# The last mixer's head loop: the second out-gate panel, the key drains and the decay scans in other places

## The reference

```
z = h @ w_in                      # q | k | v | out_gate
g = log_sigmoid(h @ down @ up + bias) / 16        # for each direction
per chunk of 64 tokens: b = cumsum(g)
  A = tril((q*exp(b)) @ (k*exp(-b)).T);  o = A @ v + (q*exp(b)) @ S
  S = exp(b_last) * S + (k*exp(b_last - b)).T @ v
o = rms_norm(o_fwd + o_bwd, g_norm) * silu(out_gate);  y = o[latent] @ w_o
```

## Time and profile before

| | us |
|---|---|
| median of 3 runs | 2536.21 (2536.12 to 2538.74) |
| profiled execution, its own time | 2537.61 |
| its span, first to last instruction | 2535.8 |
| mean granted TensorE clock | 0.988 |
| TensorE busy | 2421.2 (95%) |
| VectorE busy | 877.4 (35%) |
| ScalarE busy | 474.6 (19%) |

### The profile page before, as it was taken

The page is one execution under the profiler, slowest core; times in us unless marked ns, Lnnn a source line. Parts: engine busy times, 40 slices in busy tenths (PEclk is TensorE's granted clock), DMA queues, the critical chain, the costliest instruction groups (busy, mean ns, idle before and its releaser), DMA issues.

```text
span 2535.8 us, 23072 instructions
## 1 busy us (share of the span) xinstructions
PE 2421.2 (95%) x9410; PEld 1611.3 (64%) x9410; DVE 877.4 (35%) x1906; ACT 474.6 (19%) x971; POOL 69.6 (3%) x101
## 2 busy tenths in 40 slices
PE   6999999999999999999999998999999989878998
PEld 4888686886478867868846554444444454547843
DVE  4663312321246532133462766810000134533001
ACT  1222320100011223010102553211100032422100
POOL 1000000000010000000000000100000001000000
PEclk9999999999999999999999999999999999989999
DMA  9753334575375333447682004541212127033431
GB/s 391 284 203 116 133 117 149 193 264 209 149 266 211 121 133 117 155 173 268 214 294 100 34 34 142 183 150 67 75 66 99 67 91 271 12 108 134 165 141 66
DMA packets 163321, 390.92 MB, mean 154 GB/s; under 512 B 6288, under 2 KB 10768, under 8 KB 160400
## 3 DMA queue, kind: packets, MB, share of 16 engines
q1 hardware_dynamic: 134400, 276.61, 30.6%
q0 software_dynamic: 26256, 102.12, 10.9%
q10 hardware_dynamic: 2560, 10.72, 1.1%
HBM read 388.37 MB, written 1.05 MB: 154 GB/s over the span
## 4 chain that ended last, share of the span: by engine, by line
PE 92%; DVE 4%; ACT 3%; issue 1%; DMA 1%; POOL 0%; DVEq 0%; ACTq 0%; POOLq 0%
PE bank L455 91%; ACT arena L1182 2%; PE bank L453 2%; DVE arena L1712 1%; DVE arena L1706 1%; DMA arena<-in_w_ada 1%; ACT arena L1185 1%; DVE arena L1709 1%; ACT L1182 0%; DVE arena L1775 0%; DVE arena L2295 0%; DVE arena L1835 0%; DVE arena L2327 0%; POOL arena L2419 0%; DVE arena L2332 0%
## 5 line engine op out<-in xcount | busy, mean ns | idle before, releaser
L455 PE MATMUL bank<-arena 128*128 128x256 f32 (+6 forms) x8922 | 2365.7, 435 | 64.3 <-DVE arena L1709 29.1
L455 PEld LDWEIGHTS bank<-arena 128*128 128x128 f32 (+2 forms) x8922 | 1554.5, 189 | 862.2 <-issue 673.9
L1712 DVE SCALAR_TENSOR_TENSOR arena<-arena 128x1028 f32<-128x1028 f32 (+6 forms) x416 | 361.1, 881 | 456.5 <-ACT arena L1182 356.4
L1706 DVE TENSOR_TENSOR arena<-bank,arena 128x512 f32<-128x512 f32 (+3 forms) x115 | 78.6, 691 | 587.7 <-PE bank L455 578.3
L1185 ACT ACTIVATE arena<-bank 128x512 f32<-128x512 f32 x227 | 127.7, 597 | 730.7 <-PE bank L455 683.2
L1182 ACT ACTIVATE arena<-arena 128x512 f32<-128x512 f32 (+7 forms) x294 | 156.4, 552 | 439.8 <-DVE arena L1787 163.1
L1706 DVE TENSOR_TENSOR arena<-arena 128x1024 f32<-128x1024 f32 (+7 forms) x233 | 94.6, 424 | 328.1 <-DMA arena<-in_post 274.4
L1182 ACT ACTIVATE arena<-bank 128x512 f32<-128x512 f32 (+1 forms) x135 | 66.1, 505 | 751.1 <-PE bank L455 750.3
L2428 POOL DMA_DIRECT2D arena<-in_w_ada x88 | 63.0, 716 | 2226.4 <-DVEq L1721 2220.3
L1712 DVE SCALAR_TENSOR_TENSOR arena<-bank,arena 128x254 f32<-128x254 f32 (+3 forms) x208 | 96.1, 501 | 51.8 <-PE bank L453 35.8
L453 PE MATMUL bank<-arena 128*128 128x128 f32 x488 | 64.2, 281 | 40.9 <-DVE arena L1709 33.2
(11 more groups left out here) (29 smaller groups left out, 105.0 us busy)
## 6 DMA issues: line engine op xcount, KB each, us to landing
arena<-in_w_ada POOLq DMA_DIRECT2D x96, 1028.0 KB, 6.9
arena<-in_w_in SPq DMA_DIRECT2D x84, 1024.0 KB, 7.3
arena<-in_w SPq DMA_DIRECT2D x60, 1024.0 KB, 7.4
arena<-in_w_mlp_in SPq DMA_DIRECT2D x32, 1024.0 KB, 7.6
arena<-in_w_mlp_out SPq DMA_DIRECT2D x32, 1024.0 KB, 7.2
arena<-in_w_gla SPq DMA_DIRECT2D x12, 1024.0 KB, 7.3
arena<-in_w_a SPq DMA_DIRECT2D x8, 1024.0 KB, 6.9
arena<-in_w_out SPq DMA_DIRECT2D x8, 1024.0 KB, 6.2
```

Source lines behind the costliest of these rows:

```text
L455: ins = nc.tensor.matmul(out, lhsT, rhs, start=start, stop=stop)
L1706: return V.tensor_tensor(out, x, y, op)
L1712: return V.scalar_tensor_tensor(out=out, in0=x, scalar=s, in1=y, op0=op0, op1=op1, **kw)
```

## The change

`GLA_PANELS` now has the second out-gate panel (column 5) last. Its two tiles leave the front: GG 2 takes the place of a key tile at the start of head 3's turn, GG 3 stands before gh(3). Z 1 goes behind the first value tile. The key panel is released in head 2 behind the last key tile, the query panel behind the last query tile.

On ScalarE the bias part of `decays` becomes `biased(h)`. The rest (exponential and logarithm) of heads 2 and 3 goes from the end of head h-2's turn into head h-1's turn, behind the drains of KK and ahead of the drain of GS0. The drains of GG 2 and GG 3 go to head 3's turn and behind it. On VectorE the magnitude becomes `magnitudes(h)` and stays at its place; the rest of `decays` for heads 2 and 3 goes into head h-1's turn behind GS1, ahead of `arguments`. VectorE now waits for GG h before it multiplies GH h.

```diff
-GLA_PANELS = [("w_gla", 0, KD, PW * i, PW) for i in (4, 5, 2, 3, 1, 0)] + \
+GLA_PANELS = [("w_gla", 0, KD, PW * i, PW) for i in (4, 2, 3, 1, 0, 5)] + \
...
@@ TensorE
-            for p in range(2):
-                w = panel()
-                for n in range(2):
-                    feature_tiles(f"GG {2 * p + n}", w, n, UT2[:, :, :T])
...
+            w = panel()
+            for n in range(2):
+                feature_tiles(f"GG {n}", w, n, UT2[:, :, :T])
...
+                    if p + tt == 0:
+                        gz_(1)
...
                     gk(h + 1)
+                    if h + 2 == G_HEADS:
+                        release(wk)
+                else:
+                    wg = panel()
+                    feature_tiles("GG 2", wg, 0, UT2[:, :, :T])
...
                     gq(h + 1)
+                    if h + 2 == G_HEADS:
+                        release(wq)
...
+            feature_tiles("GG 3", wg, 1, UT2[:, :, :T])
+            release(wg)
             gh(G_HEADS - 1)
-            release(wk + wq)
@@ ScalarE
                 if h + 1 < G_HEADS:
                     gk(h + 1)
+                else:
+                    gg(2)
                 for b in range(2):
...
                     drain(f"KK {h} {b}", flat(gKK[:, 4 * b:4 * b + n, :])).then_inc(act_done, AC.drained(f"KK {h} {b}"))
+                if 0 < h < G_HEADS - 1:
+                    decays(h + 1)
                 act.wait_ge(pe_done, PE.at(f"GS0 {h} full"))
...
                 if h + 2 < G_HEADS:
-                    decays(h + 2)
+                    biased(h + 2)
+            gg(3)
             gate_row("g1", 0)
@@ VectorE
+                if 0 < h < G_HEADS - 1:
+                    decays(h + 1)
                 dve.wait_ge(pe_done, PE.at(f"GO {h} full"))
...
                 if h + 2 < G_HEADS:
-                    decays(h + 2)
+                    magnitudes(h + 2)
+                dve.wait_ge(act_done, AC.at(f"GG {h} drained"))
                 dve.wait_ge(pe_done, PE.at(f"GH {h} full"))
```

More of the change, by code:

```diff
@@ L1067, in gz_ @@
                     mm(ps[:, :], w_up[32 * d:32 * d + 16, h * P:h * P + P], gDT[32 * d:32 * d + 16, :], done=key)
-            for p in range(2):
-                w = panel()
-                for n in range(2):
-                    feature_tiles(f"GG {2 * p + n}", w, n, UT2[:, :, :T])
[L1073 to L1080, removed]
+            w = panel()
+            for n in range(2):
+                feature_tiles(f"GG {n}", w, n, UT2[:, :, :T])
+                if n == 0:
+                    ps = open_tile("DN")
+                    for k in range(KD):
+                        mm(ps[:64, :], w_down[:, k, :], UT2[:, k, :], start=(k == 0), stop=(k == KD - 1),
+                           done="DN" if k == KD - 1 else None)
+                else:
+                    gz_(0)
+            release(w)
             for p in range(2):
@@ L1605, in _, with biased @@
                 modulated2("X", j, 4, 0)
-            def decays(h):
+            def biased(h):
                 if h:
@@ L1614, in decays @@
                         act_done, AC.drained(f"Z {h} {d}"))
+            def decays(h):
                 lo = gL[:, h % 2, :, :].rearrange("p a b -> p (a b)")
@@ L1632, in exponentials, with gg @@
                 func(gdec[:, :, 0:4], gends[:, h % 2, :, :], ACT.Exp, scale=1.0 / G_TAU).then_inc(act_done, AC.step(f"gexp {h}"))
-            for j in range(4):
+            def gg(j):
                 act.wait_ge(pe_done, PE.at(f"GG {j} full"))
                 drain(f"GG {j}", flat(gOT[:, 2 * j:2 * j + 2, :]), ACT.Silu).then_inc(act_done, AC.drained(f"GG {j}"))
[L1637 to L1642, removed]
+            gg(0)
+            act.wait_ge(pe_done, PE.at("DN full"))
+            ps = tile("DN")
+            func(gDT[:64, :], ps[:64, :], ACT.Copy).then_inc(act_done, AC.drained("DN"))
+            gg(1)
+            biased(0)
+            decays(0)
             for p in range(2):
@@ L1646, in _ @@
                     drain(f"GV {p} {tt}", gV[:, tt, PW * p:PW * p + PW]).then_inc(act_done, AC.drained(f"GV {p} {tt}"))
+                    if p + tt == 0:
+                        biased(1)
+                        decays(1)
             def gk(h):
@@ L2279, in chunked, with magnitudes @@
                 return x.rearrange("p (c s) -> p c s", s=G_CHUNK)
-            def decays(h):
+            def magnitudes(h):
                 z, lo = gZ.rearrange("p a b -> p (a b)"), gL[:, h % 2, :, :].rearrange("p a b -> p (a b)")
@@ L2287, in decays @@
                 stt(lo, z, -1.0, z, ALU.mult, ALU.max).then_inc(dve_done, DV.step(f"gabs {h}"))
+            def decays(h):
+                z, lo = gZ.rearrange("p a b -> p (a b)"), gL[:, h % 2, :, :].rearrange("p a b -> p (a b)")
                 dve.wait_ge(act_done, AC.at(f"gln {h}"))
@@ L2342, in _ @@
                 if n < 2:
+                    magnitudes(n)
                     decays(n)
```

## The result

The changed kernel takes 2517.88 us (median of 4 runs, 2517.43 to 2518.43) against 2536.16 us (4 runs, 2535.88 to 2538.74): a ratio of 0.9923 with a 95% interval of 0.9912 to 0.9935, 18.3 us less. Forecast were 2515.8 us and a range of 2511.5 to 2523.5. The profiled execution took 2518.26 us, 19.35 less than the one before.

A forecast was written before the change was run, and what follows sets the result against it. The head loop was taken as bound by a VectorE and ScalarE chain. Gains of 13.7 us to gh(0), 17.6 to gh(1), 21.4 to gh(2), 22.4 in all, less 2.0 for the clock, left 20.4: 2515.8 us, range 2511.5 to 2523.5.

The forecast's parts named there:

- Front: Mixer up to gh(0): two gate tiles of 6.86 us leave, so everything there comes 13.72 us earlier.
- slack before head 0: Before head 0: its products end at 2152.0, TensorE wants them at 2153.0, leaving 1.0 us.
- Head chain: ghn h to ghn h+1, h = 1, 2: one VectorE and ScalarE chain of 22.5 us, each 3.85 us shorter.
- Panels on SP: Weight loads on SP's queue: loading the gate panel later and releasing keys and queries in head 2 cost nothing.
- Last stretch: From gh(2) to the out-projection: 18.2 us in place of 19.2.
- Clock: Granted clock: one fall of 3.4 us at half rate, plus 0.3 for a second, costs 2.0 us; bounds 0 and 5.1.
- What follows behind 2286.8 is the same work: Behind the out-projection's end: the same work as before, so no term was counted there.
- A: Rival, 13%: head chain holds, front doesn't; late conditioning weights or costlier ScalarE order take 5.6 us: gain 14.8, 2521.4.
- B: Rival, 11%: no falls of the clock at all, since no wait exceeds 4.1 us: gain 22.4, 2513.8.
- C: Rival, 2%: a table load holds the next activation back by as much again, 5.1 us: gain 15.3, 2520.9.
- D: Rival, 2%: slower; the clock does not come back between heads, TensorE at 1.2 GHz from gh(0) costs 53 us: 2569.
- E: Rival, 4%: GG 2 fills the long wait but ghn 2 comes later by as much; only 2 x 3.85 remain: 2528.5.

The follow-up runs named there:

- e8: Changed kernel with value tile GV 1 3 made in two halves, ahead of key tiles 2 and 3, head 0's arguments left behind all twelve conditioning turns: 2523.33 us.
- e5: Changed kernel with 2, 3 and 3 idle identity matmuls on TensorE in the waits before gh(0), gh(1) and gh(2): 2516.95 us.
- e6: Changed kernel with the logarithm replaced by a second exponential, so one table load goes and the result is not the reference's: 2513.70 us.
- e9: Changed kernel with VectorE's decays and scans ahead of GS1 in place of behind it: 2521.07 us.
- e3: Changed kernel with key and query panels held until after the last head, as before the change: 2522.77 us.
- e4: Changed kernel with one tiny square root behind the two gate row drains, loading the square root's table early: 2518.00 us.
- e7: Changed kernel with GV 1 3 in two halves, head 0's arguments and products behind the tenth and eleventh conditioning turns, and the root's table loaded early: 2512.29 us.
- e11: The changed kernel measured and profiled again, unaltered: 2517.83 us (5 runs).
- e1: Changed kernel with only the second gate panel's move, the ScalarE and VectorE order taken back to that of the kernel before: 2522.77 us.
- e2: Kernel before with only the new ScalarE and VectorE order, panels untouched: 2531.52 us.
- e10: e7 with four idle identity matmuls on TensorE in the wait before gh(2): 2511.47 us.

## Why the prediction was right

- *Front.* 13.72 forecast, 13.82 measured. The slack before head 0: products end at 2152.95 (2152.80 + 0.15 in DVE's order), PE comes at 2154.06, 1.1 us; forecast 1.0. The arguments ended at 2145.34, 87.0 us behind the mixer's first product as against 87.2 before: the shift, given as -1 to +3, was none, and cost nothing. e8 confirms that nothing more was to be had without DVE's order.
- *Head chain.* 22.5 forecast, 22.63 measured. For head 2, 23.03: the excess of 0.4 is the fall of the clock (e5: 22.60). e6 shows that the links count one to one, e9 that the place beside GO counts, 3.2 us in the median against 4 expected.
- *Panels on SP.* "Both cost nothing" is right for the kernel as it is. Not seen was that the release in head 2 is needed: without it the third held panel costs 5.1 us up to the out-projection's end (e3).
- *Last stretch.* 1.0 us less forecast without a fall (19.2 to 18.2), 0.8 measured, at the upper clock.
- *Clock.* The one fall came, but behind the wait of 2.77 and not that of 4.1, in the chain-bound part; it cost 0.4, not the 1.7 taken. The wait before gh(2) was 2.78 in place of 4.1, because PE's work of head 2 was slowed in front of it. In e4 and e7, where nothing fell earlier, it is 3.95 and the fall follows it. So one fall of 3.4 us was the right count at the wrong place, and the 2.0 us taken for it was 1.6 too much.
- *The term that was mis-sized.* "What follows behind 2286.8 is the same work": the work is, but not the state of ACT's table. The sum noted the load before head 3's root and hid it rightly, and did not follow the table one step on, where silu leaves it for the root of the mix. 1.0 us in the ledger, 1.15 by the waits, counted as 0 (e4).
- *Luck.* Up to the out-projection's end the forecast was 20.4 and the ledger has 21.7; behind it 0 and -1.0. The clock counted too dear and the table not counted offset each other, so that the total of 20.6 lies within 0.2 of the forecast is luck; that each link came within 0.1 to 0.5 is not.
- *From profile to median.* Forecast gain 20.4; the stretch gave 20.6, the profiles 19.35 and the medians 18.3, those of e11 21.2 against the runs beside it. The 2.9 us between the last two are the medians of the kernel before. In profiled executions of the same code such differences lie at the mixer's start; that they do so in the others is likely and not shown, for they left no trace.
- *Rivals.* A: front and chain held as in the rows. B: a fall came. C: the load costs 1.28 and the period moved by 1.1 to 1.2 (e6). D: the clock comes back after 3.4 us. E: ghn 2 came with the chain, not with GG 2 (e1).

## What to carry to other kernels

Where an engine waits, write down the whole chain that ends the wait, link by link; moving work of the waiting engine into the wait and shortening the chain are two gains, and here they added, but for where the clock fell (1.6 us, e1 and e2). Before moving work out of a front part, ask which stream there keeps its own pace (here the conditioning weights) and where the next consumer stands in the order behind it: in e8 a shorter front came back as a wait of 6.2 us, and in e7, with head 0's arguments and products moved ahead of the last turns, there was none. A moved activation takes its function table along: follow the table to the next function, not only to the next instruction. And a difference of about 1 us counts only between landmarks near the change, with the granted clock beside it.

## What was not expected of the hardware

A fall of the granted clock to 1.2 GHz for 3.4 us cost 0.43 us in a stretch that other engines bound (e5) and 1.3 to 1.6 us in one that PE bound (e4 against e5, 47.09 and 45.75; e7 against e10, 47.38 and 45.75). Idle products in the waits kept the clock at 1.00 from gh(0) to the out-projection's end in both kernels that had them (e5, e10), but where the chain set the period this bought next to nothing.

The length of the wait alone does not tell whether a fall follows: behind 2.77 us before gh(1) the clock fell in the kernel after and in e11, and behind 2.76 us at the same place in e4 it did not. What decides between them stays open here.
